# Two attention heads of a pair issued alternately on TensorE, in the score matmuls and the value products

## What is computed

```python
s = jnp.einsum('bqhd,bjkhd->bhqjk', qr, kb).astype(jnp.float32) * scale
s = s + bias                                   # learned, by relative position
s = jnp.where(col_mask, s, -jnp.inf)
p = jax.nn.softmax(s.reshape(B, H, GRID_W, wr * GRID_W), axis=-1)
return jnp.einsum('bhqn,bnhd->bqhd', p, vb)
```

## Time and profile before

| | before |
|---|---|
| median of 3 runs | 881.25 us |
| profiled execution: span, first to last instruction (the page gives no other time of it) | 880.9 us |
| TensorE matmul busy | 862.5 us (98%) |
| VectorE busy | 638.4 us (72%) |
| ScalarE busy | 404.7 us (46%) |
| mean granted TensorE clock | 0.996 of full |
| DMA | 174 GB/s mean |

### The profile page before, as it was taken

One profiled execution on the slowest core, in us unless ns is written; L12 is line 12 of the kernel. 1 busy time (PEld: TensorE's weight loads), 2 busy tenths in 40 slices (PEclk: granted clock), 3 DMA queues, 4 the chain that ended last, 5 costly groups with the idle time before them and its releaser, 6 DMA issues.

```text
span 880.9 us, 14529 instructions
## 1 busy us (share of the span) xinstructions
PE 862.5 (98%) x4913; PEld 742.2 (84%) x4913; DVE 638.4 (72%) x1304; ACT 404.7 (46%) x667; POOL 45.7 (5%) x51
## 2 busy tenths in 40 slices
PE   6999999999999999999999999999999999999995
PEld 5888888888888888888888888888888888888884
DVE  4866776885787688678858877886786687774444
ACT  5553444536435444534444354444344455544442
POOL 5400001000100000010000001000000000000002
PEclk9999999999999999999999999999999999999998
DMA  8956657666656656566566556565566777666532
GB/s 238 289 162 167 186 144 184 168 167 166 161 162 168 158 158 181 151 166 177 145 186 164 165 163 166 155 178 145 151 180 172 211 191 191 191 239 212 196 117 96
DMA packets 270966, 153.44 MB, mean 174 GB/s; under 512 B 15240, under 2 KB 261088, under 8 KB 270304
## 3 DMA queue, kind: packets, MB, share of 16 engines
q1 hardware_dynamic: 269936, 149.17, 61.2%
q10 hardware_dynamic: 1008, 3.98, 1.2%
HBM read 151.04 MB, written 2.10 MB: 174 GB/s over the span
## 4 chain that ended last, share of the span: by engine, by line
PE 95%; DMA 1%; SPq 1%; DVE 1%; ACT 0%; POOL 0%; DVEq 0%; issue 0%; ACTq 0%
PE psum L959 51%; PE psum L961 25%; PE psum L1027 3%; PE psum L1150 3%; PE psum L1151 3%; PE psum L1152 3%; PE psum L1012 2%; DMA raw<-in_w_in 1%; SPq L266 1%; PE psum L1003 1%; PE psum L1040 1%; PE psum L985 1%; PE psum L986 0%; PE psum L987 0%; PE psum L1032 0%; PE psum L994 0%
## 5 line engine op out<-in xcount | busy, mean ns | idle before, releaser
L959 PE MATMUL psum<-act_hl,w_hi 128*128 128x512 f32 x1664 | 595.8, 401 | 0.3 <-DVE w_lo L596 0.3
L961 PE MATMUL psum<-act_hl,w_lo 128*128 128x256 f32 x1664 | 465.0, 279 | 0.0
L959 PEld LDWEIGHTS psum<-act_hl,w_hi 128*128 128x128 f32 x1664 | 312.4, 188 | 79.1 <-DVE w_lo L596 3.7
L596 DVE TENSOR_TENSOR w_lo<-raw,w_hi 128x1024 fp32r<-128x1024 f32 x270 | 319.3, 1222 | 75.4 <-ACT w_hi L386 75.1
L961 PEld LDWEIGHTS psum<-act_hl,w_lo 128*128 128x128 f32 x1664 | 314.0, 189 | 0.0
L386 ACT ACTIVATE w_hi<-raw 128x1024 fp32r<-128x1024 f32 x272 | 272.8, 1051 | 32.7 <-PE psum L1152 25.7
L397 ACT ACTIVATE part<-psum 128x256 f32<-128x256 f32 x104 | 39.6, 381 | 279.0 <-PE psum L961 279.0
L959 PE MATMUL psum<-branch_hl,w_hi 128*128 128x512 f32 x256 | 90.7, 399 | 0.0
L961 PE MATMUL psum<-branch_hl,w_lo 128*128 128x256 f32 x256 | 71.9, 281 | 0.0
L613 DVE TENSOR_TENSOR hg<-psum,part 128x256 f32<-128x256 f32 x40 | 16.9, 422 | 57.3 <-ACT part L397 57.3
L959 PEld LDWEIGHTS psum<-branch_hl,w_hi 128*128 128x128 f32 x256 | 48.1, 188 | 12.2 <-DVE branch_hl L762 0.3
(11 more groups left out here) (128 smaller groups left out, 589.1 us busy)
## 6 DMA issues: line engine op xcount, KB each, us to landing
raw<-in_w_in SPq DMA_DIRECT2D x104, 1024.0 KB, 5.7
raw<-in_w_branch SPq DMA_DIRECT2D x16, 1024.0 KB, 6.1
raw<-in_w_out SPq DMA_DIRECT2D x16, 1024.0 KB, 5.1
bias_t<-in_na_rel_bias SPq DMA_DIRECT2D x32, 96.0 KB, 5.4
big<-in_x SPq DMA_DIRECT2D x2, 1024.0 KB, 6.3
big<-in_x ACTq DMA_DIRECT2D x2, 1024.0 KB, 6.7
out<-big SPq DMA_DIRECT2D x5, 256.0 KB, 2.7
wide<-in_norm_post_w ACTq DMA_DIRECT2D x1, 1024.0 KB, 4.7
```

The source lines that it names most:

```text
L596: nc.vector.tensor_tensor(w_lo[:, i, :], raw[:, r, 1024 * h:1024 * (h + 1)], w_hi[:, i, :].bitcast(F32), ALU.subtract).then_inc(lo_ready, 1)
L959: nc.tensor.matmul(sums[h][:, :], w_hi[:, i, w], operand[:, k, :], start=first, stop=False, skip_group_check=True)
L961: ins = nc.tensor.matmul(sums[h][:, 0:T], w_lo[:, i, w], operand[:, k, 0:T], start=False, stop=last, skip_group_check=True)
```

## The change

Head 1's scores go to the bank `ps_pt` instead of `ps_s` (`ps_heads`). `both_scores` replaces the two calls of `head_scores`: in slot 2 it issues the twelve score matmuls in one block, one of head 0 and one of head 1 in turn. It waits for both banks to have been taken in the group before. `turn_prob(g, 0)` also waits until VectorE has taken the scores of both heads. `heads_out` replaces the two calls of `head_out`: in slot 7 it issues the four value products in one block, in the order head 0, head 1, head 0, head 1. The number of matmuls, their shapes and their data stay as they are. VectorE reads head 1's scores from the other bank, in the same place of its order.

```diff
+        ps_heads = (ps_s, ps_pt)
@@ scores_and_max
-                nc.vector.scalar_tensor_tensor(out=pv, in0=ps_s[:, :].rearrange("p (u k) -> p u k", u=2),
+                nc.vector.scalar_tensor_tensor(out=pv, in0=ps_heads[a][:, :].rearrange("p (u k) -> p u k", u=2),
@@
-            def head_scores(g, a):
+            def both_scores(g):
                 pe.wait_ge(qk_lo_ready, g + 1)
-                wait(pe, s_taken, g * 2 + a)
-                rows = slice(HEAD * a, HEAD * (a + 1))
+                wait(pe, s_taken, g * 2)
+                wait(pe, pt_taken, g * 2)
                 for u in range(2):
                     t = 1 - u
...
+                    for i, (left, right) in enumerate(((qk_hi, qk_hi), (qk_hi, qk_lo), (qk_lo, qk_hi))):
+                        for a in range(2):
+                            rows = slice(HEAD * a, HEAD * (a + 1))
+                            ins = nc.tensor.matmul(ps_heads[a][:, u * T:(u + 1) * T], left[rows, q], right[rows, k],
+                                                   start=(i == 0), stop=(i == 2))
+                            if (u, i) == (1, 2):
+                                ins.then_inc(s_done, 1)
@@ turn_prob
+                if a == 0:
+                    pe.wait_ge(s_taken, g * 2 + 2)
@@
-            def head_out(g, a):
-                pe.wait_ge(pt_taken, g * 2 + a + 1)
+            def heads_out(g):
+                pe.wait_ge(pt_taken, g * 2 + 2)
                 pe.wait_ge(tr_taken, g * 2 + 1)
                 wait(pe, oa_ready, g)
                 for kt in range(2):
...
+                    for a in range(2):
+                        cols = slice(HEAD * a, HEAD * (a + 1))
+                        ins = nc.tensor.matmul(ps_o[cols, 0:T], v_tok[:, kt, cols],
+                                               prob_t[:, a, kt * T:(kt + 1) * T], start=(kt == 0), stop=(kt == 1))
+                ins.then_inc(pv_done, 1)
@@ attention
                 if s == 2:
-                    head_scores(g, 0)
+                    both_scores(g)
                 if s == 3:
...
-                    head_scores(g, 1)
@@
                     turn_prob(g, 1)
-                    head_out(g, 0)
                 if s == 7:
-                    head_out(g, 1)
+                    heads_out(g)
```

More of the change, by code:

```diff
@@ L975, in turn_x @@
                 ins.then_inc(xt_done, 1)
-            def head_scores(g, a):
+            def both_scores(g):
                 pe.wait_ge(qk_lo_ready, g + 1)
-                wait(pe, s_taken, g * 2 + a)
-                rows = slice(HEAD * a, HEAD * (a + 1))
+                wait(pe, s_taken, g * 2)
+                wait(pe, pt_taken, g * 2)
                 for u in range(2):
                     t = 1 - u
[L984 to L988, removed]
+                    q, k = slice(t * P, (t + 1) * P), slice(T, 2 * T)
+                    for i, (left, right) in enumerate(((qk_hi, qk_hi), (qk_hi, qk_lo), (qk_lo, qk_hi))):
[5 more added lines that the diff above has]
+                                ins.then_inc(s_done, 1)
             def turn(v, g, i):
```

## The result

The changed kernel took 861.08 us (median of 4 runs, 860.45 to 861.94) against 882.06 us for the kernel before on the same chip. The ratio is 0.9766, 95% interval 0.9754 to 0.9778, so the kernel became 2.2 to 2.5% faster. A second comparison, with five runs, gave 0.9777 [0.9764, 0.9791]. The gain was 21.0 us in the first and 19.1 us in the second; the forecast was a gain of 16.6 us, to 864.6 us, in a range from 860.5 to 878.5 us.

A forecast was written before the change was run, and what follows sets the result against it. TensorE was taken as the bound. Per group 0.39 + 0.70 + 0.33 + 0.65 = 2.07 us saved, 16.6 us over eight groups, from 881.25 to 864.6 us; range 860.5 to 878.5 us.

The forecast's parts named there:

- The bound: Eight groups run at TensorE's pace, never idle in a 78.61 us group; VectorE has 17.9 us to spare in each.
- what it was said to hide: VectorE would not notice head 0's scores up to 0.70 us later; `pv_done` up to 0.86 us later is covered.
- only the scores: Rival: score matmuls of two heads overlap, value products do not; gain 1.42 us a group, 869.9 us; chance 0.20.
- only the values overlap: Rival: value products of two heads overlap, scores do not; gain 1.37 us a group, 870.3 us; chance 0.06.
- the one in which nothing does: Rival: alternation gives nothing, only two saved ways in and out count; 875.5 us; chance 0.23.
- One block in place of two: Score and value blocks: one way in and out of each kind saved, 0.39 and 0.33 us a group.
- The scores side by side: Score block: head 1's matmuls run beside head 0's, six steps of 0.117 us instead of twelve; 0.70 us a group.
- the loads of both heads queue for one path: Rival for the score block: twelve weight loads at 0.11 us take 1.3 us, as the matmuls do now; gain zero.
- The values side by side: Value block: an in-order queue overlaps partly, 5 steps of 0.215 us instead of 8; 0.65 us a group.
- The pace: Projections run at 0.347 or 0.352 us a pair; altered blocks may shift it, zero in the sum, ±4 us in range.
- The base: The sum starts from the median 881.25 us; the span of 880.9 us was put 0.35 us under it.
- The slower rival: Each change of tile inside a block waits, 0.20 us (scores) or 0.165 us (values); +16 us, 897 us; chance 0.15.

The follow-up runs named there:

- same_rows: Changed kernel, but both score matmuls of a pair read rows 0 to 63, so head 1's scores come from head 0's data; 866.96 us, ratio 0.9830.
- values_full: Changed kernel, but the value products use all 128 columns for each head, head 0's first, without narrow tiles; 866.01 us, ratio 0.9820.
- merged: Changed kernel without alternation: in both merged blocks all of head 0's matmuls come before head 1's; 864.54 us, ratio 0.9803.
- extra_block: Changed kernel with four more full-array transposes of a constant in slot 5 of every group, results not used; 865.32 us, ratio 0.9809.
- alternated: The changed kernel itself, with matmuls of head 0 and head 1 in turn; 861.08 us, ratio 0.9766.
- threes: Changed kernel with the scores in runs of three, head 0 then head 1, twice; 860.16 us, ratio 0.9751.
- fours: Changed kernel with the scores in runs of four, four, two and two, head 0 and head 1 in turn; 861.61 us, ratio 0.9782.

## Why the prediction was right, and where its sizes were off

**The bound.** TensorE stayed busy for 76.01 of 76.01 us in a group, and each block's saving came out whole in the group (1.20 and 1.30 us for the two parts of the change, 0.1 us of each by the pace). VectorE, with 15 us to spare, hid what it was said to hide, and no wait on w_lo or L668 was added. With a gain from each part, the rivals in which only the scores or only the values overlap fall, and so does the one in which nothing does.

**One block in place of two.** Forecast 0.39 and 0.33 us a group. same_rows gives 0.38 us for the scores; for the values 1.20 − 0.86 = 0.34 us. That this belongs to narrow tiles is shown by values_full, where it is gone.

**The scores side by side.** Forecast 0.70 us, measured 0.71 us (same_rows against the changed kernel). The rival in which the loads of both heads queue for one path at 0.11 us each falls: the loads start in pairs. The 0.11 us of L1047 is a pace within one tile. By what the Trainium skill says in "TensorEngine Tiling (Array Packing)", Key Properties, on different tiles loading and multiplying in parallel, the trace now agrees: six steps in place of twelve (same_rows has the twelve).

**The values side by side.** This is the term that was mis-sized: 0.65 us, from five steps in an in-order queue, measured 0.86 us, four steps. merged shows why: between two tiles, matmuls don't start in the order of issue. "TensorE: Matmul & The Clock Gate", The mechanism, in the Trainium skill says that matmuls start and end strictly in program order; for the starts the measurement decides against it, since in merged one starts ahead of three that were issued before it. The ends are modelled in the profile and show nothing either way. 0.21 us a group are 1.7 us in all, half of the 3.5 us between forecast and result.

**The pace.** Put in as 0 ± 4 us, with 0.352 us a pair read from four pairs; over whole slow halves it is 0.354, which would have made it ± 5 us. It was 0.3 us a group, about 2.1 us over seven full groups, in favour of the change. Its sign could not be foreseen from what I knew, so that the kernel lies 2 us lower by it is luck, and its cause is still open: extra_block shows that a small block turns it, not why. In the full groups of the traces before and after, of the blocks of four L1027 or L1034 alone every third at most has a slow half behind it. The branch stage shows 1.6 us more of it as chance from one execution to the next. The group came out at 76.01 us, not 76.5: 0.21 us by the values and 0.31 us by the pace. Both errors had the same sign, so the result lies only 0.6 us above the lower end of the range.

**The base.** The prediction sets the span of 880.9 us beside the median time of 881.25 us. In each run on record the time of an execution is 1.7 us over its span, so the profiled execution of before was one of some 882.6 us (an estimate), with the slow branch stage. The sum starts from the median and doesn't depend on this.

**The slower rival.** A change of tile within the block costs nothing that can be seen: eleven of them and three, as issued (alternated, threes), give 0.89 and 0.90 us.

## What to carry to other kernels

Where TensorE is the bound, price a small block from start to start, its neighbours included: about a third of one head's block here was the way into and out of narrow tiles, and it is paid once for each block, not for each matmul. Put matmuls of different rows or columns of the array next to each other with results in different banks or partitions, and their even steps halve. Strict alternation wasn't needed here: with the partner up to four places behind, the overlap was full; with six it was not. If a change moves small blocks, the pace of everything between them may shift as well (here 2.1 us of 881 in favour of the change, and 0.1 us a group against it in extra_block), so compare block by block before believing the total.

## What the runs showed of the hardware that was not expected

- Between two tiles TensorE starts matmuls out of the order of issue: the fifth with the first (values in merged, scores in fours), the seventh only with the third (scores in merged). Within the first pair the second starts 0.003 us later when it stands one place behind, 0.013 us when it stands four behind.
- Float32 value products (two instructions for each matmul) overlap as fully as the float32r scores: eight instructions in four steps of 0.215 us.
- Identical projection matmuls run at 0.347 or 0.354 us a pair, carried from half to half, turned by the small blocks, and in the branch stage different from one execution to the next (89.13 or 90.79 us).
